# Gate path computed turned, turnings spread over it, the context's attention last

## The reference

```python
parts, gate = modulate_project(x, mod, w_in)   # u @ w_in: queries, keys, values, z of each branch
qa, ka = rope(rms_norm(...))                   # branch A; branch C (window) has no norm
# A: attention over all keys and a cache; C: over a band of blocks and the cache, with a sink
s = einsum('bkgqd,bksd->bkgqs', q, k) * HEAD_DIM ** -0.5
o = einsum('bkgqs,bksd->bkgqd', softmax(s), v)
# context tokens attend to context keys alone: one block of 128 queries and 128 keys per head
merged = sum(sigmoid(g) * ((y * silu(z)) @ w_branch) for the branches A, B, C)
h = alpha * x + gate * (merged @ w_out); x = layer_norm(h) * ln_g + ln_b
```

## Time and profile before

| what | value |
|---|---|
| median of three runs | 1681.0 us (1677.06 to 1683.05) |
| the profiled execution | 1683.48 us |
| its span | 1681.7 us |
| TensorE busy | 1553.0 us, 92% of the span |
| VectorE, GpSimd, ScalarE busy | 765.6, 628.8, 471.6 us |
| mean granted clock of TensorE | 0.973 |

### The profile page before, as it was taken

How to read it: one execution, slowest core, us unless ns; L and a number is a source line. 1 busy time by engine, 2 the same in 40 slices (tenths; PEclk the granted TensorE clock), 3 DMA queues, 4 the chain that set the end, 5 groups by cost and what they waited for, 6 DMA issues and landing times.

```text
span 1681.7 us, 22070 instructions
## 1 busy us (share of the span) xinstructions
PE 1553.0 (92%) x8803; PEld 1249.4 (74%) x8803; DVE 765.6 (46%) x1468; ACT 471.6 (28%) x1099; POOL 628.8 (37%) x504
## 2 busy tenths in 40 slices
PE   3797999998999999999979889999889999999997
PEld 2686778886588887788757777788757888767876
DVE  3268740356702362622495867006483236143246
ACT  0123740136610032311023267101463002233010
POOL 2164015530135544146761500455011554422571
PEclk9899999998999999999989999999899999999999
DMA  9121002223612212124430100122130222211421
GB/s 327 54 79 50 1 13 76 75 63 130 201 42 85 75 53 74 32 63 175 117 100 38 54 26 1 50 76 76 38 116 26 75 76 63 63 57 30 171 76 63
DMA packets 75991, 128.68 MB, mean 77 GB/s; under 512 B 16173, under 2 KB 20721, under 8 KB 75889
## 3 DMA queue, kind: packets, MB, share of 16 engines
q1 hardware_dynamic: 72416, 118.88, 22.5%
q10 hardware_dynamic: 3472, 8.39, 1.3%
HBM read 120.96 MB, written 6.30 MB: 76 GB/s over the span
## 4 chain that ended last, share of the span: by engine, by line
PE 78%; DVE 12%; issue 3%; ACT 3%; POOL 1%; DMA 1%; ACTq 1%; POOLq 0%; DVEq 0%
PE pb L942 58%; PE pb L1170 4%; PE pb L967 3%; PE pb L1122 2%; PE pb L1085 2%; PE pb L1093 1%; PE pb L898 1%; PE pb L1207 1%; DMA raw<-in_w_mod 1%; DVE xh L2404 1%; ACTq L1409 1%; PE pb L1344 1%; DVE xh L2412 1%; ACT prc L1551 1%; DVE xh L2395 1%
## 5 line engine op out<-in xcount | busy, mean ns | idle before, releaser
L942 PE MATMUL pb<-wsp,act_T 128*128 128x512 f32 x3480 | 812.1, 392 | 11.8 <-DVE act_T L1866 11.8
L942 PEld LDWEIGHTS pb<-wsp,act_T 128*128 128x128 f32 x3480 | 654.0, 189 | 151.7 <-issue 16.4
L795 POOL CAST wsp<-raw 128x1024 fp32r<-128x1024 f32 x132 | 142.9, 1083 | 881.9 <-PE pb L942 745.0
L798 POOL TENSOR_TENSOR wsp<-raw,wsp 128x512 fp32r<-128x512 f32 x280 | 374.6, 1359 | 24.4 <-ACT wsp L1436 13.9
L942 PE MATMUL pb<-wsp,yT 128*128 128x512 f32 x720 | 165.2, 389 | 0.0
L942 PEld LDWEIGHTS pb<-wsp,yT 128*128 128x128 f32 x720 | 135.1, 188 | 28.1
L2364 DVE SCALAR_TENSOR_TENSOR mt<-tg,pb 128x512 f32<-128x512 f32 x40 | 27.4, 685 | 257.7 <-PE pb L942 256.9
L1725 ACT ACTIVATE tg<-pb 128x512 f32<-128x512 f32 x60 | 36.0, 600 | 357.6 <-PE pb L942 357.6
L1573 ACT ACTIVATE pr<-pb,nm 128x640 f32<-128x640 f32 (+2 forms) x128 | 91.5, 715 | 4.4 <-DVE nm L2048 4.4
L2364 DVE SCALAR_TENSOR_TENSOR merged<-tg,pb 128x512 f32<-128x512 f32 x20 | 13.8, 688 | 147.2 <-PE pb L942 147.2
L1122 PE MATMUL pb<-ident,pr 128*128 128x128 f32 x480 | 75.5, 279 | 2.2 <-ACT pT L1610 1.9
(11 more groups left out here) (275 smaller groups left out, 1882.8 us busy)
## 6 DMA issues: line engine op xcount, KB each, us to landing
raw<-in_w_in SPq DMA_DIRECT2D x112, 512.0 KB, 3.5
raw<-in_w_mod SPq DMA_DIRECT2D x32, 512.0 KB, 4.5
raw<-in_w_branch SPq DMA_DIRECT2D x24, 512.0 KB, 3.6
raw<-in_w_out SPq DMA_DIRECT2D x16, 512.0 KB, 3.6
stage<-in_w_mod ACTq DMA_DIRECT2D x8, 512.0 KB, 16.3
stage<-in_w_mod SPq DMA_DIRECT2D x8, 512.0 KB, 11.9
raw<-in_w_in SPq DMA_DIRECT2D x16, 256.0 KB, 5.0
xh<-in_x_sample SPq DMA_DIRECT2D x7, 512.0 KB, 7.0
```

The lines of the kernel that those rows point to most:

```text
L795: pool.tensor_copy(hi, raw[:, p % 3, :, 0:width]).then_inc(raw_hi, 1)
L798: ins = pool.tensor_tensor(lo[:, j, :], raw[:, p % 3, j, 0:width], hi[:, j, :].bitcast(F32), ALU.subtract)
L942: mm = pe.matmul(dst, lhs(a, k, t), w[:, wa, j, 0:width], start=(k == 0 and n == 0), stop=(i == count - 1 and j == 1 and n == 2))
```

## The change

The gate path is computed turned. For each of four chunks `c` of 128 gate columns the weight is the loaded operand and the activations are streamed, 2 x 320 tokens, into two banks. The result is `zT` itself. All four pieces have to be there at once; pieces 0 and 1 go to the buffers `T1` and `T2`. The turnings of keys and queries stand between the 16 steps of this loop, the last tile of queries in step 1 of the attention's loop. The context's scores move to step 32 of the loop, its turning and its values between the pieces of the projection `G`; C's `gates()` follows them there. In C the values run eight steps behind the scores instead of seven. Branch A's rotation takes tables that hold the gains (`rope2`, three operations once a layer in place of one a tile). In layer 1 queries 1 to 3 are prepared ahead of the loop.

```diff
-PV_AFTER = PT_AFTER + 4
-STEPS = NL + PV_AFTER + 3
+PV_AFTER = {"A": PT_AFTER + 4, "C": PT_AFTER + 5}
+STEPS = {br: NL + PV_AFTER[br] + 3 for br in PV_AFTER}
+Z_STEPS = [(c, i) for two in ((0, 1), (2, 3)) for part in ((0, 1), (2, 3)) for c in two for i in part]
+Z_BANKS = (0, 2, 0, 6)
+def z_turns(l, br):
+    if (l, br) == (1, "A"):
+        return {3: ("qT", 0, 4), 5: ("qT", 1, 6), 8: ("kT", 0, 4), 9: ("kT", 1, 5), 10: ("kT", 2, 2),
+                11: ("kT", 3, 3), 12: ("kT", 4, 2), 13: ("kT", 5, 3), 14: ("qT", 2, 4), 15: ("qT", 3, 4)}
+    return {2: ("kT", 0, 4), 3: ("kT", 1, 5), 4: ("kT", 2, 6), 5: ("kT", 3, 7), 6: ("kT", 4, 4),
+            7: ("kT", 5, 5), 8: ("qT", 0, 4), 10: ("qT", 1, 2), 13: ("qT", 2, 2), 15: ("qT", 3, 4)}
...
 GpSimd
-            for t in range(3, T):
-                of_q(0, t)
+            of_q(0, 3)
             split(z[3])
+            of_q(0, 4)
...
 TensorE, attention
-                    project((br, "z"), after=keys)
-                    for t in range(T):
-                        pe.wait_ge(q_ready[l], bi * T + t + 1)
-                        transpose_blocks((br, "qT", t), ...)
-                        wait_done(pe, (br, "z", t))
-                        transpose_blocks((br, "zT", t), lambda i: zt[:, t, tile_cols(i)], 4)
+                    def gate_path():
+                        first, turns = pieces.first[l, (br, "z")], z_turns(l, br)
+                        for n, (c, i) in enumerate(Z_STEPS):
+                            p, key = first + i, (br, "z", c)
+                            if p not in split_seen:
+                                pe.wait_ge(raw_used, pieces.order[p] + 1)
+                                split_seen.add(p)
+                            if i == 0:
+                                acquire(key)
+                            w, b = split_of(p), bank_of(key)
+                            for j in range(2):
+                                k = 2 * i + j
+                                for m, (a, wa) in enumerate(((0, 0), (0, 1), (1, 0))):
+                                    for h in range(2):
+                                        mm = pe.matmul(pb[:, b + h, 0:320], w[:, wa, j, tile_cols(c)],
+                                                       act_T[:, a, k, h * 320:(h + 1) * 320], ...)
+                            ...
+                            if n in turns:
+                                turned(*turns[n][:2])
...
-                    for s in range(STEPS):
-                        if s == 0:
-                            scores_context()
+                    for s in range(STEPS[br]):
                         if s < NL:
                             scores(s)
                         if s == 1:
-                            probs_context()
+                            turned("qT", LT)
+                        if s == NL:
+                            scores_context()
                         if 0 <= s - PT_AFTER < NL:
                             probs_T(s - PT_AFTER)
-                        if s == 3:
-                            values_context()
...
+                    def context(i, t):
+                        if (i, t) == (0, T - 1):
+                            probs_context()
+                        if (i, t) == (1, T - 1):
+                            values_context()
+                        if br == "C" and (i, t) == (2, T - 1):
+                            gates()
...
 ScalarE, attention (layer 0 and C)
-                        for t in range(T):
-                            if t < 2:
-                                hi_part(2 + t)
-                            if t == 2:
-                                k_turned()
-                            q_rounded(br, t)
+                        hi_part(2)
+                        q_rounded(br, 0)
+                        hi_part(3)
+                        turned("kT", 0)
+                        q_rounded(br, 1)
...
+                        if s in (NL, NL + 1):
+                            exponent_context(s - NL)
...
 VectorE, attention (layer 0 and C)
+                        q_path(br, 0)
+                        q_path(br, 1)
+                        q_lo(br, 0)
+                        q_path(br, 2)
+                        q_lo(br, 1)
+                        gate_z(0)
+                        q_path(br, 3)
+                        q_lo(br, 2)
+                        gate_z(1)
+                        q_path(br, 4)
+                        q_lo(br, 3)
+                        q_lo(br, 4)
+                    gate_z(2)
+                    gate_z(3)
...
 ScalarE, end of layer 0
-                    hi_piece(pieces.first[1, ("A", "z")])
-                    hi_piece(pieces.first[1, ("A", "z")] + 1)
                     of_kv(4)
+                    hi_piece(pieces.first[1, ("A", "z")])
+                    hi_piece(pieces.first[1, ("A", "z")] + 1)
```

More of the change, by code:

```diff
@@ L124, in __init__, with add @@
         self.turn = 0
[L126 removed]
+    def add(self, layer, key, matrix, blocks, *columns, slots=None, of=None, by_act=False, last=T - 1):
         self.first[layer, key] = len(self.items)
@@ L341, in plan_layer @@
                     psum.roll((br, name, hf, t))
+                if br != "B" and (name, hf) == ("G", 0):
+                    keys = [(br, "PTctx", 0), (br, "PTctx", 1), (br, "Octx")]
+                    for key in keys:
+                        psum.roll(key)
+                    if br == "C":
+                        for i in range(4):
+                            psum.take(("gate", i), psum.use[l, keys[i % 3]][0])
                 if (br, name, hf) == ("B", "G", 0):
```

338 lines of the change are left out of this document (189 added, 149 removed).

## The result

The changed kernel takes 1654.07 us (median of four runs, 1652.62 to 1658.49), the kernel before beside it 1679.19 (1677.06 to 1683.05): the ratio is 0.9852, with a 95% interval of 0.9824 to 0.988. It is 25 us faster; 20 were forecast.

A forecast was written before the change was run, and what follows sets the result against it. TensorE, busy 92% of the span, was taken as the bound. 46.2 - 14.8 - 9.6 - 6.8 + 5 = 20 us off the profiled 1683.5 gave 1663.5, 2.5 over the median, so 1661 us; range 1640 to 1678.

The forecast's parts named there:

- what bounds the kernel: Whole kernel: TensorE, busy 92% of the span; work taken from other engines counts only where TensorE waits for it.
- the heads: Start of z to third unit's scores, A and C in both layers: gains 10.9, 14.3 and twice 10.5, sum 46.2 us.
- the waits for pieces: A's gate path: TensorE waits for GpSimd's pieces of z, 5.9 us in layer 0 and 3.0 in layer 1.
- the pause at A's end: End of A's loop: context exponents between ScalarE's copies make the last values 4.5 us later, 2.7 of it waiting.
- The rival of a free end: Loop's end: new waits and the lower clock behind them don't come, 16.4 us more kept, 1645 us; chance 0.25.
- The clock behind the pause: After each loop-end pause TensorE runs at the lower clock for the first 3 us: 1.7 us each, 6.8 in all.
- the end of C: End of C's loop, both layers: last values 3.9 us later, 2.1 of it waiting, plus 1.7 us of clock.
- A's sum: End of A's loop: scores, maximum, exponents, cast, copies and hand-overs add to 8.4 us before the last values.
- the values' step: C's late loop: values one step later remove half of TensorE's idle, 0.14 us a unit, 5 us, bounds 0 and 10.
- given back: Loop ends: moved context work 14.8 us, waiting 9.6, lower clock 6.8; the values' step gains 5.
- The slower rival: Gate path: weight loads of 320-column matmuls not hidden, 87 us more, 1748 us; this or another such loss 0.08.
- The starving gate path: Gate path: turnings wait for VectorE or pieces, layer 0 and C each add 3 to 4 us, 1676 us; chance 0.17.

The follow-up runs named there:

- e4: Changed kernel with pieces of z split earlier on GpSimd (layer 0) and rounded earlier on ScalarE (both layers): 1656.53 us, ratio 0.9852.
- e7: Changed kernel with e2's and e4's edits, and in layer 1 piece 1 of z split ahead of the keys' root: 1631.14 us, ratio 0.9711.
- e2: Changed kernel with ScalarE's eight context exponents behind the copy of unit 31's probabilities, VectorE's normalising behind its loop: 1642.19 us, ratio 0.9771.
- e1: Changed kernel with C's values back at seven steps behind the scores, nothing else: 1655.88 us, ratio 0.9863.
- e8: Changed kernel with the edits of e7 and e6 together: 1628.54 us, ratio 0.97.
- e9: e8 with C's values back at seven steps behind the scores: 1635.19 us, ratio 0.9728.
- e6: Changed kernel with GpSimd's splitting of the first pieces of C's G held back until unit 30's scores, both layers: 1653.17 us, ratio 0.9834.
- e10: Changed kernel with the context back at the loop's head and C's values at seven steps, leaving the turned gate path: 1671.17 us, ratio 0.9939.

## Why the prediction was right, and where it was not

**Right: what bounds the kernel, and the heads.** From z's start to the third unit I had forecast 44.7 us in layer 0's A, 40.5 in layer 1's and 37.6 in C; measured are 44.4, 965.41 - 925.66 = 39.8, and 37.3 in both C. The sum of the heads is 46.7 us against 46.2. (C's 37.3 count the pause of 0.73 us that stands ahead of z's first matmul, as the forecast did.) Errors cancel in it. A matmul of 320 columns costs 0.150 us where 24 stand in a row (the next instruction starts at 147.59, so 3.61 us for the row at 143.98), not 0.146, so the layout costs 1.6 us a time (192 x 0.150 less 27.2) instead of 0.8; the waits for pieces are 4.8 and 2.6 us instead of 5.9 and 3.0, and the third unit waits 0.38 us in A where 1.2 and 0.9 were put down. That GpSimd's order of roots and pieces makes the waits for pieces is shown by e4 and e7.

**Right: the pause at A's end.** The last values come 11.64 - 7.16 = 4.5 us later in both layers, as forecast. That the exponents between the copies make it is shown by e2. The rival of a free end was priced at 16.4 us; taking the exponents away gave 11.9, so it would have been about right as a kernel of its own, and it named the change worth making next. TensorE's idle time is 3.49 us; the 3.9 in the forecast don't follow from its own terms, which give 0.82 + 2.7 = 3.5. The clock behind the pause cost about 1.3 and 1.6 us in A (last values and first half of `G` together 33.1 and 33.45 us; e2, with the same instructions there and a pause of 0.82, takes 31.8); 1.7 were forecast.

**Wrong in size: the end of C.** Forecast were 3.9 us later and 1.7 us of clock in each. Measured are 1.4 and 2.9 us later, and of clock nothing in layer 0 and 1.6 in layer 1 (last values and first half of `G` 34.8 and 36.4 us, in e2 34.8 in both). The step at fault is "In C the same sum gives 3.9 us": it carries A's sum over and leaves out that C's values stand one step further behind, which the same change does. Without that step (e1) they come 3.0 and 5.0 us later. It also takes the two layers for equal, and the kernel before already lost clock at the end of layer 0's C. Windows of before, from unit 31's scores to the last values, layer 0 and layer 1:

```profile
457.48:465.94 8.46, 6.09 (x36) 3.73 (x34) 5.19 (x18) 5.96 (x16) 0.00 (x0) 0.80 0.20 64
...
1269.84:1276.33 6.49, 4.57 (x36) 2.81 (x35) 4.47 (x15) 5.05 (x13) 0.00 (x0) 1.00 0.01 3
```

**Wrong: the values' step.** Forecast were 5 us inside the loops, from half of the idle time in the earlier trace rows. The step gave the loops nothing. They are shorter by 6.7 us in all, of which 4.1 are the context's values that left them (1.0 each), and by 9.3 without the step (e1). What the step gives stands at the ends: about 1.8 us in the changed kernel, where it shortens waits for ScalarE's copies (e1), and 5 to 7 in e8, where it covers part of a wait for VectorE that the late splits have stretched (e9). That every unit passes through all three engines was a reason for the idle to stay, not for half of it to go.

**The sum.** Forecast were 46.2 less 26.2 given back (14.8 + 9.6 + 6.8 - 5). Measured between the profiled executions is 46.7 less 19.8: the ends take 26.5 us instead of 31.2, all of the difference in C, and the loops give 6.7 instead of 5. That the loops come out near is luck. The sum books the context's values at the ends (within the 14.8) and doesn't take them out of the loops, where they stood behind the third unit; these 4.1 us stand in for the 5 that the step didn't give. Another 4.0 us lie behind the last attention's branch product (372.8 us to the end of the span before, 368.8 after), which nobody forecast and no run explains. So the profiled executions differ by 30.9 us. That of before lies 4.3 over its median, where the forecast took 2.5, and that of the changed kernel 1.4 under its own: 25 us between the medians against 20.

**The slower rival fell.** It decided from 0.172 us a matmul on, and the rows show 0.150 with a load for each, which leaves 0.017 us beside the stream's 320 / 2.4 GHz = 0.133. The rule of the Trainium skill behind it ("TensorE: Matmul & The Clock Gate", section on packing small matmuls) doesn't hold for these rows, as with 512 columns. The starving gate path fell too: it was priced at 15 us, and no wait in the gate paths is over 2.59 us.

**What the prediction did not see** is that its parts hang together. It summed the gate path and the context's move into one gain per head. Alone they give 8.8 and 2.9 us: the gate path leaves the wait for the context's exponents, and the move pays at the ends what it saves at the heads. The effect of the rotation tables and of the early queries in layer 1 was not measured.

## What to carry to other kernels

Work moved off the head of a loop takes its latency with it: look on the engine that runs in strict order for what it lands between, and put it behind the last operation that anyone waits for. Price the parts of a change alone and together, since a part that clears one of two waits in a row gives little until the other goes too. And when a gain of a few microseconds doesn't show in the time, cut both timelines at the same instructions: in e4 some of it was gone 290 us later, at a pause after which the clock fell, as it didn't in the profiled execution of the changed kernel.

## What the hardware showed that I had not expected

Beside GpSimd's splitting, some of VectorE's operations take three to nearly nine times as long, while a maximum read from PSUM doesn't stretch (0.68 us for 128 x 512 numbers at 434.70 in the changed kernel, 0.69 at 428.14 ahead of the splitting): in the rows above 0.42 us becomes 1.19 for scaling 128 x 384 numbers in SBUF, and an addition of 128 x 1 numbers takes 1.22 us beside the splitting and 0.14 after it. The Trainium skill says why ("SBUF — State Buffer", section "SBUF: two separate sides"): the two engines share a pair of ports under an exclusive lock, held for the whole instruction. The trace agrees, since the small addition was held about as long as one of GpSimd's subtractions of 128 x 512 lasts (2.52 us for two), and e6 shows it by moving the splits: the stretch follows them.

Whether the clock falls behind a pause is not settled by the pause's length alone: behind 3.29 us in layer 0's C it stayed at 1.00, behind 3.05 us at the same place in e4 it was 0.50, at 1.2 GHz. Behind 2.59 us in layer 1's A, 36 matmuls took 5.55 us in the changed kernel and 7.09 in e10. In A's ends it fell behind 3.49 us in both layers, and behind 0.82 us it did not; in layer 0's C it was at 0.53 in e2 and 0.89 in e7 over the same instructions. What decides it, no run here shows.
